# Reversed column order in the float32r products of a two-block decoder kernel, with the split weights at four relative places

## Chip, cores and metric

One core of a Trainium2 chip runs the whole program in one launch. The metric is the device time of that core in microseconds (us), from the first to the last instruction with what lies around them. Lower is better.

## What is computed

The reference is one layer of a hybrid decoder (a gated delta rule and a Mamba-2 mixer side by side, then a gated feed-forward with a short convolution), followed by a second block of two mixers (stick-breaking attention with multi-scale pooling; gated linear attention), each with its own feed-forward. There are 512 positions of 1,024 channels, in float32. Cut to what matters here:

```python
def hybrid_layer(x, ...):
    h = rms_norm(x, pre_mix_norm)
    proj = h @ w_in                                   # 1024 -> 6688
    ...                                               # delta rule and SSD, chunks of 64
    x = x + rms_norm(concatenate([o_a, o_s]) @ w_out, post_mix_norm)      # 2048 -> 1024
    h = rms_norm(x, pre_ffn_norm)
    u = causal_dwconv(h @ w_up, ffn_conv_w, ffn_conv_b)                   # 1024 -> 2 * 2816
    gate, up = split(u, 2)
    return x + rms_norm((silu(gate) * up) @ w_down, post_ffn_norm)        # 2816 -> 1024
# second block: an even mixer, a feed-forward, an odd mixer, a feed-forward,
# with the same kinds of products
```

Nearly all of the arithmetic is in these products of a weight matrix with an activation matrix of 512 columns.

## The kernel before

**Layout.** Activations lie channels by positions: a tile is 128 channels (partitions) by 512 positions, and a tensor of 1,024 channels is `KD` = 8 such tiles side by side. A weight matrix is cut into units. A unit makes 128 output channels: it is the stack of the 128x128 blocks that meet the input's tiles, 8 of them for an input of 1,024 channels (`KD`) and 11 for half of the 2,816 channels of the feed-forward (`HALF`). There are 305 units in the program.

**Exactness by splitting.** Both factors are split into two float32r parts, high and low. ScalarE rounds a unit to `whi` (L187), VectorE takes the remainder to `wlo` (L193), and the activations have such pairs too: `HH` and `HL`, `FH` and `FL` in the feed-forward, `MH`/`ML`, `PH`/`PL` and `DH`/`DL` in the mixers. TensorE then does three matrix products a block: high by high, high by low, low by high (L255 to L257 in `multiply`), and adds them up in one PSUM bank. Each is a weight load of 128x128 and a matmul that reads 512 columns of the activation tile (the moving operand) and writes 512 float32 columns of the bank. So a unit of `KD` is 24 matmuls, one of `HALF` 33.

**Where else the same product stands.** `fan` (L231 to L233) does two or three units side by side as the tiles of a normalised activation arrive, `begin_pe` (L1466 to L1468) does the same for the very first two units, and `mix_pe` (L2634 to L2636) is the output product of the first mixer. `busy` (L220) issues matmuls on split weights whose result nobody reads.

**The queue of weights.** SyncE loads each unit from HBM into one of four buffers `raw` (`RAW` = 4) once the unit four before it has been split. `whi` and `wlo` are two buffers each (`SPLIT` = 2), used in turn, so unit u + 2 is split when unit u is done (semaphore `unit_done`). Some units are split into tiles of their own ahead of time (`first_weights`, `early`).

**Places in SBUF.** `fixed` hands out addresses one after the other: parameters, `X`, `HH`, `HL`, four `raw`, two `whi`, two `wlo`, the constants `cst` (15 blocks of 128x128), `small`; all later tiles lie at `FREE` and beyond. A row of `whi` is 11 x 128 x 4 = 5,632 bytes, 11 times 512, and the tiles at `FREE` start a multiple of 512 bytes from `HH`. So every weight block and every activation tile that meet in a product start at the same remainder modulo 512 bytes.

**Order.** Each engine's instructions are written out stage by stage by hand; waits are on semaphores that count upward. What the change touches on the queues is the load of the constants in `load_l1`, L2190, behind the fourth weight unit. The semaphore `params_in` has counted all such loads when it reaches `ALL_PARAMS` = 16 x 9; TensorE waits for that at L1456, ScalarE and VectorE at the start of the first mixer (L2653, L2660).

## Time and profile before

| | |
|---|---|
| time of two runs | 2145.89 and 2153.01 us, median 2149.45 us |
| the profiled execution's own time | 2152.09 us |
| its span, first to last instruction | 2150.3 us |
| mean granted TensorE clock | 0.993 of full speed |
| instructions in the span | 26,841 |
| TensorE matmul (PE) | 2102.0 us busy, 98%, 9,776 |
| weight load (PEld) | 1702.9 us, 79%, 9,776 |
| VectorE (DVE) | 1212.8 us, 56% |
| ScalarE (ACT) | 905.8 us, 42% |
| GpSimd (POOL) | 325.0 us, 15% |
| DMA, share of 16 engines | 0.28, 88 GB/s |

How to read it. All times are of one execution. A row of the timeline gives the start of an instruction in us from the span's start, its duration, the engine, the line of the kernel, the operation and the names of what it writes and reads. The matmul's duration there contains the latency of a pipeline (0.39 us), while the next one starts 0.23 us after it: what a stream of matmuls costs is read from start to start. "128*128 128x512" is the size of the weights, and then what moves through them. PE and PEld are the same engine; the load for the next matmul runs beside the present one.

### The profile page before, as it was taken

The numbers are of one execution on the slowest core, as the hardware profiler recorded it, in microseconds if no ns is written. First come the engines' busy times: TensorE is split into PE (matmuls) and PEld (weight loads), VectorE is DVE, ScalarE is ACT, GpSimd is POOL, SyncE is SP. The second block draws the span as 40 slices with busy tenths as digits, with TensorE's granted clock in tenths as the row PEclk, the third lists the DMA queues.
The fourth block names the chain that finished last, engine by engine and source line by source line (L and its number), as shares of the span: only waits on it lengthen the run. The fifth ranks groups of instructions, "written<-read, shape, count | busy, mean of one in ns | idle before, by whom it ended". The sixth has DMA issues, their size and how long they took to land.

```text
span 2150.3 us, 26841 instructions
## 1 busy us (share of the span) xinstructions
PE 2102.0 (98%) x9776; PEld 1702.9 (79%) x9776; DVE 1212.8 (56%) x1663; ACT 905.8 (42%) x1282; POOL 325.0 (15%) x266
## 2 busy tenths in 40 slices
PE   6999999999999999999999999999999999999999
PEld 5778888878868888887766888888878878888887
DVE  5898755755366666225544566653354465666522
ACT  6883444434254444224555444442242254444421
POOL 0001121210112222001302122220000012222200
PEclk9999999999999999999999999999999999999999
DMA  7323222122223333222211333232222122333321
GB/s 235 93 77 93 75 75 79 49 69 69 91 66 98 98 98 115 99 80 69 66 43 40 98 98 96 93 119 95 86 69 89 60 70 97 98 97 96 116 95 66
DMA packets 81481, 188.96 MB, mean 88 GB/s; under 512 B 19824, under 2 KB 40432, under 8 KB 81392
## 3 DMA queue, kind: packets, MB, share of 16 engines
q1 hardware_dynamic: 81392, 187.75, 27.7%
q8 instruction: 59, 0.97, 0.2%
q14 instruction: 30, 0.25, 0.0%
HBM read 178.28 MB, written 9.44 MB: 87 GB/s over the span
## 4 chain that ended last, share of the span: by engine, by line
PE 91%; DVE 5%; ACT 2%; issue 1%; DMA 0%; POOL 0%; SPq 0%; DVEq 0%; ACTq 0%
PE acc L255 23%; PE acc L257 23%; PE acc L256 23%; PE bank L1247 1%; PE bank L231 1%; PE bank L233 1%; PE bank L232 1%; PE acc L2636 1%; PE acc L2634 1%; PE acc L2635 1%; PE bank L2019 1%; PE bank L1728 1%; DVE wlo L193 1%; PE bank L255 1%; PE bank L256 1%
## 5 line engine op out<-in xcount | busy, mean ns | idle before, releaser
L255 PE MATMUL acc<-HH,whi 128*128 128x512 f32 x1600 | 643.6, 402 | 6.9 <-DVE wlo L193 4.3
L257 PE MATMUL acc<-HH,wlo 128*128 128x512 f32 x1600 | 625.7, 391 | 0.0
L256 PE MATMUL acc<-HL,whi 128*128 128x512 f32 x1600 | 624.7, 390 | 0.0
L187 ACT ACTIVATE whi<-raw 128x1024 fp32r<-128x1024 f32 (+1 forms) x293 | 324.0, 1107 | 566.1 <-PE acc L257 536.8
L193 DVE TENSOR_TENSOR wlo<-raw,whi 128x1024 fp32r<-128x1024 f32 (+1 forms) x293 | 400.8, 1369 | 283.0 <-ACT whi L187 283.0
L255 PEld LDWEIGHTS acc<-HH,whi 128*128 128x128 f32 x1600 | 301.9, 189 | 73.8 <-DVE wlo L193 10.3
L257 PEld LDWEIGHTS acc<-HH,wlo 128*128 128x128 f32 x1600 | 301.2, 188 | 64.2
L256 PEld LDWEIGHTS acc<-HL,whi 128*128 128x128 f32 x1600 | 302.0, 189 | 62.6 <-issue 4.1
L255 PE MATMUL acc<-FH,whi 128*128 128x512 f32 x528 | 205.8, 390 | 0.0
L256 PE MATMUL acc<-FL,whi 128*128 128x512 f32 x528 | 205.4, 389 | 0.0
L257 PE MATMUL acc<-FH,wlo 128*128 128x512 f32 x528 | 205.4, 389 | 0.0
L390 DVE TENSOR_TENSOR acc<-acc,rs 128x512 f32<-128x512 f32 x150 | 104.8, 698 | 175.7 <-PE acc L257 175.7
L482 POOL TENSOR_TENSOR taps<-taps,taps 128x512 f32<-128x512 f32 x66 | 85.3, 1292 | 507.5 <-DVE taps L468 452.5
L447 ACT ACTIVATE FH<-taps 128x512 f32 (+1 forms) x66 | 41.8, 633 | 199.3 <-POOL taps L482 199.3
L255 PEld LDWEIGHTS acc<-FH,whi 128*128 128x128 f32 x528 | 99.1, 188 | 20.9 <-issue 0.2
L256 PEld LDWEIGHTS acc<-FL,whi 128*128 128x128 f32 x528 | 99.1, 188 | 20.8 <-issue 0.2
L257 PEld LDWEIGHTS acc<-FH,wlo 128*128 128x128 f32 x528 | 99.1, 188 | 20.5
L345 POOL TENSOR_TENSOR hn<-hn,sq 128x512 f32<-128x512 f32 x24 | 36.7, 1528 | 410.9 <-ACT sq L338 410.9
L468 DVE SCALAR_TENSOR_TENSOR taps<-acc,par,taps 128x510 f32<-128x510 f32 x117 | 87.6, 749 | 14.7 <-DVE taps L464 0.5
L487 POOL TENSOR_TENSOR FL<-taps,FH 128x512 f32 (+1 forms) x66 | 85.5, 1295 | 59.9 <-ACT FH L447 59.9
L438 ACT ACTIVATE taps<-acc,par 128x512 f32<-128x512 f32 x117 | 89.0, 761 | 0.6 <-DVE acc L390 0.6
L464 DVE SCALAR_TENSOR_TENSOR taps<-acc,par,taps 128x511 f32<-128x511 f32 x117 | 86.6, 740 | 0.0
(394 smaller groups left out, 2674.4 us busy)
## 6 DMA issues: line engine op xcount, KB each, us to landing
raw<-w SPq DMA_DIRECT2D x257, 512.0 KB, 3.5
raw<-w SPq DMA_DIRECT2D x48, 704.0 KB, 4.0
X<-x SPq DMA_DIRECT2D x4, 512.0 KB, 5.2
x_dram<-small SPq DMA_DIRECT2D x8, 256.0 KB, 4.7
xt_dram<-small SPq DMA_DIRECT2D x8, 256.0 KB, 4.5
a_dram<-l_am SPq DMA_DIRECT2D x8, 256.0 KB, 3.6
l_xt<-xt_dram SPq DMA_DIRECT2D x8, 256.0 KB, 3.3
l_x<-x_dram SPq DMA_DIRECT2D x8, 256.0 KB, 3.1
```

Source lines behind the costliest of these rows:

```text
L187: nc.scalar.activation(hi[:, 0:kt * P], raw[u % RAW][:, 0:kt * P], ACT.Copy).then_inc(w_hi_ready, 1)
L193: nc.vector.tensor_tensor(lo[:, 0:kt * P], raw[u % RAW][:, 0:kt * P], hi[:, 0:kt * P].bitcast(F32), ALU.subtract).then_inc(w_lo_ready, 1)
L255: nc.tensor.matmul(a[:, :], wh, tile(hi, k), start=start and k == 0, stop=False)
L256: nc.tensor.matmul(a[:, :], wh, tile(lo, k), start=False, stop=False)
L257: last = nc.tensor.matmul(a[:, :], wl, tile(hi, k), start=False, stop=stop and k == kt - 1)
L390: nc.vector.tensor_tensor(a[:, :], a[:, :], rs[:, :], ALU.mult).then_inc(scaled, 1)
L438: nc.scalar.activation(taps[j][:, :], a[:, :], ACT.Identity, scale=w(2), bias=w(3)).then_inc(tap_ready, 1)
L447: nc.scalar.activation(o, taps[j - 1][:, :], ACT.Copy).then_inc(fh_ready, 1)
L464: nc.vector.scalar_tensor_tensor(out=taps[j][:, 1:S], in0=a[:, 0:S - 1], scalar=w(1), in1=taps[j][:, 1:S], op0=ALU.mult, op1=ALU.add).then ...
L468: nc.vector.scalar_tensor_tensor(out=taps[j][:, 2:S], in0=a[:, 0:S - 2], scalar=w(0), in1=taps[j][:, 2:S], op0=ALU.mult, op1=ALU.add).then ...
L482: nc.gpsimd.tensor_tensor(taps[2 * b][:, :], taps[2 * b][:, :], taps[2 * b + 1][:, :], ALU.mult).then_inc(prod_ready, 1)
L487: nc.gpsimd.tensor_tensor(o, taps[2 * b][:, :], h.bitcast(F32), ALU.subtract).then_inc(f_ready, 1)
```

## The change

In the products named above, both the activation tile that is read and the PSUM bank that is written are given as `t[:, ::-1]`: the same elements with a step of -1, starting at column 511. Column j of the input still makes column j of the output. `busy`, and all products in plain float32, keep their order. The weight blocks are read as before.

The split weights get a row that is one block longer (12 x 128), and a unit starts in it at a shift: 0 or 64 elements for the units of 8 blocks (0 or 256 bytes, by buffer), 32 or 96 elements for those of 11 (128 or 384 bytes). The units with tiles of their own (`first_weights`, `early`) stay at shift 0.

To make room, `cst` shrinks from 15 to 10 blocks. The five left out (part of `level`) aren't read in the kernel before either. `FREE` moves down by 512 bytes.

```diff
-        whi = [fixed(f"whi{j}", [P, HALF * P], F32R) for j in range(SPLIT)]
-        wlo = [fixed(f"wlo{j}", [P, HALF * P], F32R) for j in range(SPLIT)]
-        cst = fixed("cst", [P, 15 * P])
+        whi = [fixed(f"whi{j}", [P, HALF * P + P], F32R) for j in range(SPLIT)]
+        wlo = [fixed(f"wlo{j}", [P, HALF * P + P], F32R) for j in range(SPLIT)]
+        SHIFT = {KD: (0, 64), HALF: (32, 96)}
+
+        def weights(w, kt):
+
+            o = SHIFT[kt][w]
+            return whi[w][:, o:o + kt * P], wlo[w][:, o:o + kt * P]
+
+        def flipped(t):
+
+            return t[:, ::-1]
+
+        cst = fixed("cst", [P, 10 * P])
...
-        NORM_COLUMNS, ALL_PARAMS = 9, 16 * 9
+        NORM_COLUMNS, ALL_PARAMS = 9, 16 * 10
...
-                wh, wl = whi[w][:, k * P:(k + 1) * P], wlo[w][:, k * P:(k + 1) * P]
-                nc.tensor.matmul(a[:, :], wh, tile(hi, k), start=start and k == 0, stop=False)
-                nc.tensor.matmul(a[:, :], wh, tile(lo, k), start=False, stop=False)
-                last = nc.tensor.matmul(a[:, :], wl, tile(hi, k), start=False, stop=stop and k == kt - 1)
+                wh, wl = (x[:, k * P:(k + 1) * P] for x in weights(w, kt))
+                nc.tensor.matmul(flipped(a), wh, flipped(tile(hi, k)), start=start and k == 0, stop=False)
+                nc.tensor.matmul(flipped(a), wh, flipped(tile(lo, k)), start=False, stop=False)
+                last = nc.tensor.matmul(flipped(a), wl, flipped(tile(hi, k)), start=False, stop=stop and k == kt - 1)
...
-                    sp.dma_start(cst[:, 2 * P:], cst_in[:, 2 * P:]).then_inc(params_in, 16)
+                    sp.dma_start(cst[:, 2 * P:5 * P], cst_in[:, 2 * P:5 * P]).then_inc(params_in, 16)
+                    sp.dma_start(cst[:, 5 * P:], cst_in[:, 10 * P:]).then_inc(params_in, 16)
```

`fan`, `begin_pe` and `mix_pe` are changed in the same way as `multiply`, and `split_hi` and `split_lo` write where `weights` says.

The only queue on which an instruction is added is SyncE's, near the start of the program. `raw` are the weights' buffers, `w` the weights in HBM, `par` and `cst` parameters and constants. Before:

```order
6 L2185 DMA raw_56<-w 128x1024
7 L2185 DMA raw_57<-w 128x1024
8 L2189 DMA par<-par 128x905
9 L2190 DMA cst<-cst 128x1664
10 L2192 DMA fold<-cst 32x32 x4
11 L2193 DMA tab_w<-w 128x8x32
12 L2185 DMA raw_54<-w 128x1024
```

The same place in the changed kernel, with its own line numbers:

```order
6 L2196 DMA raw_56<-w 128x1024
7 L2196 DMA raw_57<-w 128x1024
8 L2200 DMA par<-par 128x905
9 L2201 DMA cst<-cst 128x384
10 L2202 DMA cst<-cst 128x640
11 L2204 DMA fold<-cst 32x32 x4
12 L2205 DMA tab_w<-w 128x8x32
13 L2196 DMA raw_54<-w 128x1024
```

One load of 1,664 columns became two, of 384 and 640, and everything behind it stands one issue later. On TensorE, VectorE, ScalarE and GpSimd the same instructions stand in the same order in both kernels.

## Rows read from the trace of the kernel before

**Rows 1.** The page: busy time by engine, granted clock by slice, the last chain.

```profile
span 2150.3 us, 26841 instructions
PE 2102.0 (98%) x9776; PEld 1702.9 (79%) x9776; DVE 1212.8 (56%) x1663; ACT 905.8 (42%) x1282; POOL 325.0 (15%) x266
PEclk9999999999999999999999999999999999999999
PE 91%; DVE 5%; ACT 2%; issue 1%; DMA 0%; POOL 0%; SPq 0%; DVEq 0%; ACTq 0%
```

**Rows 2.** The page's DMA issues: weight units of 8 and of 11 blocks.

```profile
raw<-w SPq DMA_DIRECT2D x257, 512.0 KB, 3.5
raw<-w SPq DMA_DIRECT2D x48, 704.0 KB, 4.0
```

**Rows 3.** Timeline of PE and PEld, units of 8 blocks, full clock.

```profile
start us, us, engine line op out<-in xcount [idle before <-releaser]
699.85 0.39 PE L256 MATMUL acc<-HL,whi 128*128 128x512 f32 x1
...
702.57 0.39 PE L256 MATMUL acc<-HL,whi 128*128 128x512 f32 x1
...
699.86 0.19 PEld L257 LDWEIGHTS acc<-HH,wlo 128*128 128x128 f32 x1
```

**Rows 4.** Timeline of PE, units of 11 blocks, full clock.

```profile
900.00 0.39 PE L257 MATMUL acc<-FH,wlo 128*128 128x512 f32 x1
...
902.72 0.39 PE L257 MATMUL acc<-FH,wlo 128*128 128x512 f32 x1
```

**Rows 5.** Timeline of PE at 1.2 GHz, the first ten products.

```profile
17.93 0.63 PE L1467 MATMUL bank<-HL,early_hi 128*128 128x512 f32 x1
...
21.77 0.63 PE L1467 MATMUL bank<-HL,early_hi 128*128 128x512 f32 x1
```

**Rows 6.** Timeline of PE, plain float32 matmuls of 512 columns, full clock.

```profile
45.47 1.88 PE L1756 MATMUL bank<-l_sq,cst 128*128 128x512 f32 x4
47.18 0.94 PE L1766 MATMUL bank<-cst,t_ld 128*128 128x128 f32 x7
```

**Rows 7.** Timeline of PE, float32r products just after a gap, full clock.

```profile
59.64 0.40 PE L255 MATMUL acc<-HH,whi 128*128 128x512 f32 x1
59.88 0.39 PE L256 MATMUL acc<-HL,whi 128*128 128x512 f32 x1
60.10 0.39 PE L257 MATMUL acc<-HH,wlo 128*128 128x512 f32 x1
...
61.49 0.39 PE L257 MATMUL acc<-HH,wlo 128*128 128x512 f32 x1
```

**Rows 8.** Two stretches: us, then busy (count) by engine, clock, DMA share.

```profile
core 0: us, PE busy (x) PEld busy (x) DVE busy (x) ACT busy (x) POOL busy (x), PEclk, DMA share, GB/s
855.00:960.00 105.00, 105.00 (x465) 86.95 (x464) 28.71 (x23) 25.71 (x26) 9.45 (x8) 1.00 0.28 93
1750.00:1850.00 100.00, 100.00 (x439) 82.08 (x438) 55.65 (x63) 41.91 (x56) 22.29 (x16) 1.00 0.31 95
```

**Rows 9.** SyncE's queue near 10 us, the load's landing, and TensorE's first reader.

```profile
9.83 0.43 SPq L2190 DMA_DIRECT2D cst<-cst  x1
12.93 1.62 SPq L2185 DMA_DIRECT2D raw<-w  x1
...
cst<-cst SPq DMA_DIRECT2D x1, 832.0 KB, 7.1
...
29.57 1.92 PE L1459 MATMUL bank<-normed_x,tab_w 128*32 128x512 f32 x16
```

**Rows 10.** Groups by line: splitting on VectorE and ScalarE, with their idle time.

```profile
L193 DVE TENSOR_TENSOR wlo<-raw,whi 128x1024 fp32r<-128x1024 f32 (+1 forms) x293 | 400.8, 1369 | 283.0 <-ACT whi L187 283.0
L187 ACT ACTIVATE whi<-raw 128x1024 fp32r<-128x1024 f32 (+1 forms) x293 | 324.0, 1107 | 566.1 <-PE acc L257 536.8 <-PE acc L2636 11.9 <-PE bank L233 8.6
```

More of the change, by code:

```diff
@@ L97, in program @@
         ident, ones, upper, lower, halves = (cst[:, k * P:(k + 1) * P] for k in range(5))
-        neg_lower, neg_ones, hidden = (cst[:, k * P:(k + 1) * P] for k in range(12, 15))
-        level = [cst[:, (5 + k) * P:(6 + k) * P] for k in range(7)]
+        neg_lower, neg_ones, hidden = (cst[:, k * P:(k + 1) * P] for k in range(7, 10))
+        level = {5 + k: cst[:, (5 + k) * P:(6 + k) * P] for k in range(2)}
         def col(name, k=0, n=1):
@@ L181, in split_hi @@
         def split_hi(act, u, i, per, kt, first=None, behind=SPLIT):
-            hi = whi[u % SPLIT] if first is None else first[0]
+            hi = (weights(u % SPLIT, kt) if first is None else first)[0]
             act.wait_ge(raw_in[u % RAW], at(16 * (u // RAW + 1), i, 16 * per // RAW))
@@ L189, in split_lo @@
         def split_lo(dve, u, i, per, kt, first=None, behind=SPLIT):
-            hi, lo = (whi[u % SPLIT], wlo[u % SPLIT]) if first is None else first
+            hi, lo = weights(u % SPLIT, kt) if first is None else first
             dve.wait_ge(w_hi_ready, at(u + 1, i, per))
@@ L224, in fan @@
             u0, n = c["u"], c["fan"]
-            w = [c["first"][j] if j < 2 else (whi[(u0 + j) % SPLIT], wlo[(u0 + j) % SPLIT]) for j in range(n)]
+            w = [c["first"][j] if j < 2 else weights((u0 + j) % SPLIT, KD) for j in range(n)]
             pe.wait_ge(w_lo_ready, u0 + n)
@@ L1311, in sb_pe @@
             pe.wait_ge(w_lo_ready, u0 + 12)
-            busy(bank[0], whi[(u0 + 11) % SPLIT], 12)
+            busy(bank[0], weights((u0 + 11) % SPLIT, KD)[0], 12)
             for i in range(NP):
@@ L2632, in mix_pe @@
                         pe.wait_ge(h_ready, c["h"] - 2 * KD + h * KD + j + 1)
-                    wh, wl = whi[w][:, j * P:(j + 1) * P], wlo[w][:, j * P:(j + 1) * P]
-                    nc.tensor.matmul(a[:, :], wh, tile(hi, j), start=h == 0 and j == 0, stop=False)
-                    nc.tensor.matmul(a[:, :], wh, tile(lo, j), start=False, stop=False)
-                    last = nc.tensor.matmul(a[:, :], wl, tile(hi, j), start=False, stop=h == 1 and j == KD - 1)
+                    wh, wl = (x[:, j * P:(j + 1) * P] for x in weights(w, KD))
+                    nc.tensor.matmul(flipped(a), wh, flipped(tile(hi, j)), start=h == 0 and j == 0, stop=False)
+                    nc.tensor.matmul(flipped(a), wh, flipped(tile(lo, j)), start=False, stop=False)
+                    last = nc.tensor.matmul(flipped(a), wl, flipped(tile(hi, j)), start=False, stop=h == 1 and j == KD - 1)
                 last.then_inc(unit_done, 1)
```

18 lines of the change are left out of this document (9 added, 9 removed).

## Prediction

> **What bounds the kernel now.** I read the page first: TensorE's matmuls are busy 98% of the span, and the chain that ended last lies on PE for 91% of it [rows 1]. The granted clock is at its upper level in every slice [rows 1]. The other engines have room: in a stretch of the last feed-forward PE is busy 100 of 100 us, VectorE 56, ScalarE 42 [rows 8]. So the time is the number of matmuls by the time from one start to the next, and I looked next for both numbers.
>
> The number: 257 weight units of 8 blocks and 48 of 11 [rows 2] make 257 x 8 + 48 x 11 = 2,584 blocks, with three products each 7,752 matmuls, all of 512 columns. These are the ones that the change touches.
>
> The pace: in a steady stretch twelve of them take 702.57 - 699.85 = 2.72 us, 226.7 ns each [rows 3]. With 11-block units it is the same, 2.72 us for twelve [rows 4]. 7,752 x 226.7 ns = 1,757 us, 82% of the span of 2150.3 us. The rest (some 390 us: plain float32 products, waits, the start) isn't touched.
>
> At 2.4 GHz, 512 columns one a cycle are 213.3 ns. So each matmul pays 13.3 ns more than its columns, 7,752 x 13.3 = 103 us in all. That is the only amount that a mere change of order and place can win back, and what it consists of decides the case. Three views bear on it.
> - At 1.2 GHz nine steps take 21.77 - 17.93 = 3.84 us, 426.7 ns each, which is 512 / 1.2 GHz and nothing more [rows 5]. The surplus is there at full speed alone, so it isn't a fixed number of array cycles a matmul.
> - Plain float32 matmuls of 512 columns take (47.18 - 45.47) / 4 = 427.5 ns a pass at the full clock, 0.8 ns above two cycles a column [rows 6]. A stream that reads its columns at half the pace has no surplus either, although it loads weights as often.
> - After a gap the pace isn't 226.7 yet: eight steps take 61.49 - 59.64 = 1.85 us, 231 ns each, single ones about 240 and 220 [rows 7]. Same shape, same line, same places; the surplus depends on how the streams stand to each other.
>
> The weight load for the next matmul begins with the present matmul, 699.86 against 699.85 [rows 3]. My reading, argued and not shown: while 128 weight columns are fetched, the fetch of the moving columns at full pace is now and then held up. Then direction and relative place may matter, for better or worse. All weights and tiles of before stand at one relative place, so the trace has no row of another, and none with a step of -1.
>
> **The change, part by part.**
> 1. Reading the moving operand from column 511 down: 7,752 times, unknown price. From below: the surplus vanishes down to the 0.8 ns of [rows 6], so -12.5 ns each, -97 us. From above: one column in two cycles as at [rows 5], +200 ns each, +1,550 us. The step has the same size and the elements are neighbours as before, so the nearest row is the present one, [rows 3]. I take 0.
> 2. Writing PSUM from column 511 down: same count, same upper bound. A direction in itself has no reason to help the write. I take 0.
> 3. The four relative places: 0, 128, 256 and 384 bytes. Units of 8 blocks have 0 or 256 (2,056 blocks, 80%), those of 11 have 128 or 384 (20%). The nearest rows for another relation of the streams are [rows 7]: 231 ns, +4.6 each if all stayed there (+36 us), and about 240 ns for the single worst step. If half of the places gained 4 ns and half lost 4, the sum would be 0. I take 0, with the four as a spread that makes either extreme less likely.
> 4. The splits write to a shifted start. Sizes are unchanged; 1,369 ns on VectorE and 1,107 on ScalarE a unit, hidden below 24 x 226.7 = 5,440 ns of TensorE, with 283 and 566 us of idle time ahead of them [rows 10]. 0. If TensorE sped up to 214 ns a step, a unit would be 5,140 ns, still far above both.
> 5. One more load on SyncE's queue: 0.43 us [rows 9], and 832 KB become 512. The load before is issued at 9.83 us and lands 7.1 us later, at 17; TensorE's first wait for all parameters is ahead of the products at 29.57 [rows 9]. 12 us of cover. The next weight unit, issued at 12.93, comes 0.4 us later; it lies behind four that are loaded already. 0; without any cover it would be 0.5 us.
> 6. `FREE` moves by 512 bytes, the same remainder: 0.
>
> Sum: 0 on the profiled execution's own time of 2152.09 us (span 2150.3, 1.8 us around it). It lies 2.6 us above the median of the runs, so I give the median, 2149 us.
>
> A rule of the Trainium skill on PSUM (PSUM — Partial Sum Buffer, Specifications) speaks against the change: lines are 8 bytes, and any access that isn't contiguous slows matmuls significantly. No row here shows such an access. If a step of -1 counts as not contiguous the sum would go by the upper bound above. The page on SBUF (SBUF — State Buffer, Specifications) gives lines of 16 bytes and wants two hits in a line; read backward, float32 still has four. By that rule the read costs nothing, and the sum stays 0.
>
> **The rivals.**
> - *The streams get out of each other's way (faster).* Both fetches then meet less often, in one direction or at a shift. For it: [rows 5 to 7], which make the surplus a matter of how streams meet. Against it: 226.7 ns to the digit in two stages whose tiles lie far apart [rows 3, 4], which looks like a pattern that settles by itself whatever the place. All of the surplus gone gives 2149 - 97 = 2052 us, half of it 2149 - 48 = 2101. It passes over 2% when the mean step falls by 43 / 7.752 = 5.5 ns, to 221. Chance 0.33.
> - *They meet more often (slower).* The mechanism and place are the same, in the 7,752 steps. If every step were as the slow start [rows 7], +36 us, 2185, still within 2%. If the surplus doubled to 26.7 ns (240 ns a step, which single steps of [rows 7] reach), +103 us, 2252. It decides once the mean passes 226.7 + 5.5 = 232.2 ns. Chance 0.18 for over 2%.
> - *A step of -1 drops to one column in two cycles (much slower).* The price is that of [rows 5], whatever causes it, on the read or on the write: 426.7 ns a step, 2149 + 1,550 = 3,700 us. For it: rows of before never do this, and at 2.4 GHz a float32 stream needs neighbours fetched together. Against it: neighbours they still are. Chance 0.12. The rule of the PSUM page named above would make it this case.
> - *Nothing changes.* The two reads don't meet at all and the 13.3 ns belong to something in TensorE that neither direction nor place touches. 2149 us; with the mixtures in item 3 this is my forecast, 0.37. The Trainium skill (TensorE: Matmul & The Clock Gate, Step-by-step: what each phase is for) says that weight load and moving operand have independent read ports, by which the load takes nothing from the running matmul. By that rule the sum is 0; rows 5 to 7 don't bear it out fully, since the surplus varies with what runs beside.
>
> **How the numbers follow.** 2% is 43 us, about what a measurement of this kernel can tell from no change. Faster 0.33, within 2% 0.37, slower 0.18 + 0.12 = 0.30. The likeliest case has its own range, 2107 to 2192 us. The range for 8 in 10 takes in nearly all of the faster rival, down to 2055, and most of the milder slower one, up to 2235; it leaves out the 0.12 of the halved pace and some 0.05 at the ends.
>
> **What would show it.** The steps from start to start in the timeline: 226.7 ns in the steady stretches means nothing changed, below 221 the faster rival, above 232 the slower, near 427 the halved pace. The down stages (11 blocks) against all others tell places 128 and 384 from 0 and 256, and successive units tell the two buffers apart. If the first products of the span, at shift 0, move as much as the rest, it is the direction and not the place. Weight loads should stay at 0.19 us and the plain float32 products at 427.5 ns. TensorE's idle time should stay where it is; new idle time on it, for `wlo`, would say that something else than the pace moved. The prediction is wrong if the mean step leaves 221 to 232 ns.

## The result, and the profile after

| | before | after |
|---|---|---|
| median of two runs | 2149.45 us | 2193.4 us (2190.98 and 2195.82) |
| ratio, 95% interval | | 1.0204 [1.0117, 1.0292] |
| span of the profiled execution | 2150.3 us | 2189.2 us |
| mean granted TensorE clock | 0.993 | 0.996 |

The changed kernel is 2% slower: the loss is clear of the noise, and whether it is more or less than 2% the interval leaves open. The forecast was 2149 us with the likeliest case "nothing changes"; 2193 us lies inside the range of 2055 to 2235 us, but by the rival named "they meet more often", which had a chance of 0.18.

From the page of the kernel after: busy time by engine, the shares of the last chain, and the two groups that split weights (busy us, mean ns, then idle us and its releasers).

```profile
span 2189.2 us, 26842 instructions
PE 2143.5 (98%) x9776; PEld 1702.0 (78%) x9776; DVE 1215.1 (56%) x1663; ACT 905.1 (41%) x1282; POOL 319.6 (15%) x266
...
PE 91%; DVE 5%; ACT 2%; issue 1%; DMA 0%; POOL 0%; DVEq 0%; ACTq 0%
...
L198 ACT ACTIVATE whi<-raw 128x1024 fp32r<-128x1024 f32 (+1 forms) x293 | 323.6, 1105 | 599.2 <-PE acc L268 568.8
L204 DVE TENSOR_TENSOR wlo<-raw,whi 128x1024 fp32r<-128x1024 f32 (+1 forms) x293 | 402.3, 1374 | 279.0 <-ACT whi L198 279.0
```

Against [rows 1] PE has grown by 41.5 us with the same 9,776 matmuls. Weight loads, VectorE and ScalarE are within 2.5 us of before, GpSimd is 5 us lower, and the shape of the chain is the same. The splits take 1,105 and 1,374 ns against 1,107 and 1,369 [rows 10]; ScalarE waits 33 us longer for TensorE, which is the slower one.

Timeline of PE after: start, duration, line, what is written and read. First the same stages as in [rows 3] and [rows 4], then the first products of the span at full clock, then two at 1.2 GHz.

```profile
699.72 0.40 PE L266 MATMUL acc<-HH,whi 128*128 128x512 f32 x1
...
702.52 0.40 PE L266 MATMUL acc<-HH,whi 128*128 128x512 f32 x1
...
899.92 0.40 PE L266 MATMUL acc<-FH,whi 128*128 128x512 f32 x1
...
902.72 0.40 PE L266 MATMUL acc<-FH,whi 128*128 128x512 f32 x1
...
22.39 0.40 PE L1477 MATMUL bank<-HH,early_hi 128*128 128x512 f32 x1
...
27.99 0.40 PE L1477 MATMUL bank<-HH,early_hi 128*128 128x512 f32 x1
```

Twelve steps take 702.52 - 699.72 = 2.80 us in units of 8 blocks (places 0 and 256 bytes), 902.72 - 899.92 = 2.80 us in units of 11 (128 and 384 bytes), and 24 steps take 27.99 - 22.39 = 5.60 us in the first products, whose weights never left place 0. All three are 233.3 ns, against 226.7 before [rows 3, 4]. At 1.2 GHz three steps take 21.24 - 19.96 = 1.28 us, 426.7 ns, as in [rows 5]:

```profile
19.96 0.63 PE L1477 MATMUL bank<-HH,early_hi 128*128 128x512 f32 x1
...
21.24 0.63 PE L1477 MATMUL bank<-HH,early_hi 128*128 128x512 f32 x1
```

**The sum.** Over the whole trace, the mean of all steps below 270 ns between two such products is 227.27 ns before (the slower starts of [rows 7] included) and 233.40 ns after: 6.13 ns x 7,752 = 47.5 us. The mean clock gives some back: 0.996 x 2189 leaves 0.004 x 2189 x 2 = 17.5 us at 1.2 GHz (twice, since the lower level is half speed), before it was 0.007 x 2150 x 2 = 30.1 us, and half of the difference of 12.6 is 6 us. 47.5 - 6 gives some 41.5, which is what PE's busy time gained; the spans differ by 38.9 us and the medians by 44. So the place of the loss is one: every product's step.

SyncE's queue at the added load, and its landing (issue us, duration; then KB and us to landing):

```profile
10.16 0.44 SPq L2202 DMA_DIRECT2D cst<-cst  x1
...
cst<-cst SPq DMA_DIRECT2D x1, 320.0 KB, 6.0
```

The second load of the constants costs 0.44 us of the queue and lands 6.0 us after its issue, at 16.2 us; [rows 9] had one load landing at 17. Longest of TensorE's waits, after (engine line waited for: us in total, times, longest):

```profile
PE bank L283 <- DVE hn L312: 11.4, 1, 11.4
...
PE acc L266 <- DVE wlo L204: 4.9, 3, 2.9
```

The longest is a change of stage, and `wlo` counts for 4.9 us, against 5.4 before; no new wait stands here.

### The profile page after: what moved, and what is told of

Its sections match the earlier page's. It is cut to its first block, busy times and chain, and to the rows that moved or that the text cites. A ratio compares the mean times of both kernels' runs of the same rounds, so it can differ in the third digit from the quotient of the medians.

```text
span 2189.2 us, 26842 instructions
## 1 busy us (share of the span) xinstructions
PE 2143.5 (98%) x9776; PEld 1702.0 (78%) x9776; DVE 1215.1 (56%) x1663; ACT 905.1 (41%) x1282; POOL 319.6 (15%) x266
## 4 chain that ended last, share of the span: by engine, by line
PE 91%; DVE 5%; ACT 2%; issue 1%; DMA 0%; POOL 0%; DVEq 0%; ACTq 0%
PE acc L266 23%; PE acc L267 23%; PE acc L268 23%; PE bank L1258 1%; PE bank L242 1%; PE acc L2647 1%; PE bank L243 1%; PE bank L244 1%; PE acc L2648 1%; PE acc L2646 1%; PE bank L2030 1%; PE bank L1739 1%; PE bank L266 1%; DVE wlo L204 1%; PE bank L267 1%
## 5 line engine op out<-in xcount | busy, mean ns | idle before, releaser
L266 PE MATMUL acc<-HH,whi 128*128 128x512 f32 x1600 | 654.8, 409 | 6.1 <-DVE wlo L204 3.8
L267 PE MATMUL acc<-HL,whi 128*128 128x512 f32 x1600 | 637.6, 398 | 0.0
L268 PE MATMUL acc<-HH,wlo 128*128 128x512 f32 x1600 | 637.3, 398 | 0.0
L198 ACT ACTIVATE whi<-raw 128x1024 fp32r<-128x1024 f32 (+1 forms) x293 | 323.6, 1105 | 599.2 <-PE acc L268 568.8
L204 DVE TENSOR_TENSOR wlo<-raw,whi 128x1024 fp32r<-128x1024 f32 (+1 forms) x293 | 402.3, 1374 | 279.0 <-ACT whi L198 279.0
L266 PE MATMUL acc<-FH,whi 128*128 128x512 f32 x528 | 210.2, 398 | 0.0
L267 PE MATMUL acc<-FL,whi 128*128 128x512 f32 x528 | 209.8, 397 | 0.0
L268 PE MATMUL acc<-FH,wlo 128*128 128x512 f32 x528 | 209.8, 397 | 0.0
```

The lines of the kernel that those rows point to most:

```text
L198: nc.scalar.activation(hi[:, 0:kt * P], raw[u % RAW][:, 0:kt * P], ACT.Copy).then_inc(w_hi_ready, 1)
L204: nc.vector.tensor_tensor(lo[:, 0:kt * P], raw[u % RAW][:, 0:kt * P], hi[:, 0:kt * P].bitcast(F32), ALU.subtract).then_inc(w_lo_ready, 1)
L266: nc.tensor.matmul(flipped(a), wh, flipped(tile(hi, k)), start=start and k == 0, stop=False)
L267: nc.tensor.matmul(flipped(a), wh, flipped(tile(lo, k)), start=False, stop=False)
L268: last = nc.tensor.matmul(flipped(a), wl, flipped(tile(hi, k)), start=False, stop=stop and k == kt - 1)
```

## The experiments

The change has three parts that touch a product: the direction of the read, the direction of the write, and the weights' place. The explanations to tell apart were: the read stream meets the fetch of weights more often when it runs backward (the mechanism of the second rival); the write to PSUM pays; the places pay. Behind them stood the question of what the surplus over 213.3 ns consists of, since a kernel that avoids it would be faster than both.

Two kinds of kernels were run. The full kernel with one part of the change was timed against the kernel before, which was run again beside it each time; the ratios are to those runs. Kernels of single forms issue long streams of one form of product on fixed tiles and nothing else; they compute nothing of the reference. Of each form, 40 products settle, then 48 are recorded as one row, whose time is 47 steps and one matmul's own 0.38 to 0.40 us. So a row of 11.04 us is (11.04 - 0.39) / 47 = 226.6 ns a step, and one of 11.36 is (11.36 - 0.40) / 47 = 233.2; the steps below are worked out from unrounded rows.

### Order alone, places alone, and the whole change again

```diff
 # order_alone: the kernel after, with
-        SHIFT = {KD: (0, 64), HALF: (32, 96)}
+        SHIFT = {KD: (0, 0), HALF: (0, 0)}
 # place_alone: the kernel after, with
-            return t[:, ::-1]
+            return t[:, :]
```

> The changed kernel with all shifts at 0: the reversed order alone, weights at one relative place. Theory A (the order of the moving read meets the weight fetch more often, whatever the place): steps of 233.3 ns as in the changed kernel, time the same as it, about 2193 us, ratio to before 1.02. Theory B (the four places did it, the order is free): steps back to 226.7 ns, time about 2149 us. Theory C (the reversed write to PSUM did it): the same as A here, so this run doesn't tell A from C.

> The changed kernel with columns in ascending order on both sides: the four places alone, and the constants' load in two parts. Theory A (order): steps of 226.7 ns, time within 0.5% of before, 2149 us. Theory B (places): steps of 233.3 ns, about 2193 us; if only some places cost, the stages with 11-block units would differ from the others. Theory C (reversed write): 226.7 ns as A.

> The changed kernel as it is, for a narrower interval beside the two others on the same chip: ratio to before 1.02 (7,752 steps of 6.7 ns more are 52 us, less what TensorE's clock gives back).

| | us | ratio to before |
|---|---|---|
| order alone | 2193.67 | 1.0202 [1.0181, 1.0223] |
| places alone | 2161.52 | 1.0036 [1.0020, 1.0051] |
| whole change again | 2189.95 | 1.0189 [1.0167, 1.0211] |

Timeline of PE, order alone, units of 11 blocks:

```profile
899.73 0.40 PE L268 MATMUL acc<-FH,wlo 128*128 128x512 f32 x1
...
902.53 0.40 PE L268 MATMUL acc<-FH,wlo 128*128 128x512 f32 x1
```

Timeline of PE, places alone: units of 8 blocks, then of 11.

```profile
700.04 0.39 PE L267 MATMUL acc<-HL,whi 128*128 128x512 f32 x1
...
702.76 0.39 PE L267 MATMUL acc<-HL,whi 128*128 128x512 f32 x1
...
899.97 0.40 PE L268 MATMUL acc<-FH,wlo 128*128 128x512 f32 x1
...
902.75 0.40 PE L268 MATMUL acc<-FH,wlo 128*128 128x512 f32 x1
```

The order alone gives all of the loss: 12 steps in 2.80 us, 233.3 ns, with all places as before. The places alone leave the units of 8 blocks at 2.72 us (226.7 ns; places 0 and 256 bytes) and lift those of 11 to 2.78 us (231.7 ns here, 232.4 over the stage; places 128 and 384 bytes). 48 units x 33 products = 1,584 products x 5.7 ns = 9 us; the spans of the two traces differ by 10.9 us, and the ratio says 8 us, from 4 to 11. The two don't add up: with the read reversed, units of 11 blocks cost 233.3 ns at place 0 and at the shifted ones.

### Single forms: read or write, lines or elements

```diff
 # bench_a, some of its forms, each in a stream of its own (mv: moving, wt: weights, a: PSUM bank)
+  L73   mm(a, wt[:, 0:P], mv[:, 0:S])                       # as before
+  L80   mm(a, wt[:, 0:P], rev(mv[:, 0:S]))                  # read reversed
+  L87   mm(rev(acc[0]), wt[:, 0:P], mv[:, 0:S])             # written reversed
+  L94   mm(rev(acc[0]), wt[:, 0:P], rev(mv[:, 0:S]))        # both, as after
+  L248  mm(acc[0][:, 0:256], wt[:, 0:P], rev(mv[:, 0:256])) # 256 columns, read reversed
+  L276  mm(a, wt[:, 0:P], grouped(mv[:, 0:S], 4))           # groups of 4 backward, inside forward
+  L304  mm(a, wt[:, 0:P], grouped(mv[:, 0:S], 4, 1, -1))    # groups of 4 forward, inside backward
+  L318  mm(a, wt[:, 0:P], mv[:, 0:2 * S:2])                 # every second element
```

> A kernel of its own that leaves out the whole computation: runs of 88 equal matmuls each, 40 to settle and 48 to read the step from start to start, one form after the other, with four short float32 passes between forms. Theory A (weight fetch against moving read): base 226.7 ns; moving read reversed alone 233.3; PSUM write reversed alone 226.7; both 233.3; weights of 64 and 32 columns cost a half and a quarter of the surplus of 13.3 ns; 256 and 384 columns of moving operand the same surplus of 13.3 (120 and 173 ns); bfloat16 about 216 in both directions; moving operand shifted, or weights shifted, by less than a block: either no difference or one that repeats with 4 or 8 elements. Other orders of the moving columns (pairs, fours, blocks of 8 or 32 in descending order) lie between 226.7 and 233.3. Theory C (write): write reversed alone 233.3, read reversed alone 226.7. Theory D (a fixed cost in the array that a reversed pattern makes larger by setup): surplus independent of weight columns, and a swap of halves costs as much as a full reversal.

Timeline of PE, one row for 48 products of each form:

```profile
38.95 11.04 PE L73 MATMUL acc<-mv,wt 128*128 128x512 f32 x48
59.61 11.36 PE L80 MATMUL acc<-mv,wt 128*128 128x512 f32 x48
80.35 11.04 PE L87 MATMUL acc<-mv,wt 128*128 128x512 f32 x48
101.02 11.36 PE L94 MATMUL acc<-mv,wt 128*128 128x512 f32 x48
547.06 5.84 PE L248 MATMUL acc<-mv,wt 128*128 128x256 f32 x48
614.72 11.36 PE L276 MATMUL acc<-mv,wt 128*128 128x512 f32 x48
698.40 11.04 PE L304 MATMUL acc<-mv,wt 128*128 128x512 f32 x48
748.53 21.83 PE L318 MATMUL acc<-mv,wt 128*128 128x512 f32 x48
```

Read row by row: the reversed read costs 6.7 ns (L80), the reversed write nothing (L87), both together as much as the read alone (L94). Reversing four elements within a group of 16 bytes is free (L304), while taking the groups backward, forward inside, costs the full 6.7 ns (L276). So it is the order of 16-byte groups that counts. Every second element takes 451 ns a step, half the pace (L318).

The price of going backward holds for 512 columns and isn't the same at other lengths. With 256 columns the reversed read took 118.4 ns (L248) against 120.0 forward, which is faster; with 384 it took 177.7 against 173.3. Forward, the surplus over the columns was 13.3 ns at 256, 384 and 512 columns alike and 16.0 at 448, so it isn't in proportion to the columns either.

The Trainium skill (SBUF — State Buffer, Specifications) gives SBUF lines of 16 bytes and wants neighbours to be read together; L304 and L276 agree with lines of that size. It asks for two hits in a line for the full rate; L318 has two in each and runs at half the pace, so for float32r the runs differ from the page. What it implied for this change, that a backward read with four hits in each line is free, holds for the elements in a line and fails for the lines' order. The Trainium skill (PSUM — Partial Sum Buffer, Specifications) has any access that isn't contiguous slow a matmul significantly; with a step of -1 on the write the runs show no cost at all (11.04 us at L87 as at L73).

In the same kernel bfloat16 products took 215.8 ns in either direction, and plain float32 ones 429.2 ns a pass in either. Shortening the weights to 64 or 32 columns, with loads of 134 and 108 ns instead of 188, gave 230.1 and 231.7 ns. A half and a quarter of the surplus had been expected; it grew, so it isn't in proportion to the weight columns fetched.

### Single forms: which places and which orders

```diff
 # bench_b: weights at 22 places forward and 32 backward, moving tiles at 4, both shifted together, and the blocks' order
+  L129  mm(a, wt[:, 32:32+P], mv[:, 0:S])
+  L136  mm(a, wt[:, 36:36+P], mv[:, 0:S])
+  L185  mm(a, wt[:, 64:64+P], mv[:, 0:S])
+  L465  mm(a, wt[:, 4:4+P], mv[:, 4:4+S])
+  L486  mm(a, wt[:, 32:32+P], mv[:, 32:32+S])
```

> A kernel of its own that leaves out the whole computation: 82 forms of the float32r matmul, 88 each, as in the first such kernel. Theory A1 (the relation of the two start addresses decides, with a period of 256 bytes): in ascending order a shift of the weights by 64, 128, 192 or 256 elements gives 226.7 ns, all others 230 to 234; shifting weights and moving operand by the same amount gives 226.7 again; moving alone by 64 or more 226.7. Reversed: 233.3 at multiples of 64, up to 236.7 between, and no place back at 226.7. Theory A2 (each operand's own alignment decides): shifting both by the same amount stays at 231 to 234. Theory A3 (some place of the reversed order is better than the ascending one): at least one of the 32 reversed shifts is below 226.7. Order of moving columns: blocks of 64 elements in descending order 226.7 by A1 (their period), blocks of 16 about 233.

Timeline of PE, the five forms above:

```profile
205.51 11.32 PE L129 MATMUL acc<-mv,wt 128*128 128x512 f32 x48
226.19 11.04 PE L136 MATMUL acc<-mv,wt 128*128 128x512 f32 x48
371.29 11.04 PE L185 MATMUL acc<-mv,wt 128*128 128x512 f32 x48
1210.02 11.36 PE L465 MATMUL acc<-mv,wt 128*128 128x512 f32 x48
1271.64 11.05 PE L486 MATMUL acc<-mv,wt 128*128 128x512 f32 x48
```

Weights 128 bytes on cost 5.8 ns (L129), weights 256 bytes on nothing (L185), and both streams 128 bytes on nothing either (L486; so with 8, 16 and 64 elements). Both streams 16 bytes on did cost, 233.3 ns (L465), and both 8 bytes on 231.1. Of the 22 places of the weights, read forward, the multiples of 256 bytes and one other (36 elements, L136) were at 226.7 ns, all others from 228.3 to 234.4; places that differ by 256 bytes gave the same step. So what counts is mostly the place of one read stream against the other, modulo 256 bytes, as theory A1 has it. L465 is what theory A2 expected, so each stream's own place has a part too. Reversed, none of 32 places was below 233.3, and some were at 236.7. At 32 elements it was 236.7 in bench_a and 233.3 here, so one form can keep two paces. Going backward over blocks of 32 columns or fewer cost 233.3; over blocks of 64 columns (256 bytes) or more, forward inside, nothing: 226.7.

```diff
 # bench_c: a moving stream that reads few lines again and again; spread weights
+  L87   mm(a, wt[:, 0:P], mv[:, 0:4].unsqueeze(1).to_broadcast([P, 128, 4]))
+  L122  mm(a, wt[:, 0:P], mv[:, 0:64].unsqueeze(1).to_broadcast([P, 8, 64]))
+  L178  mm(a, wt[:, 0:8 * P:8], mv[:, 0:S])
```

> A kernel of its own that leaves out the whole computation: 45 forms, 88 matmuls each. Theory A (the surplus comes from the fetch of weights and the fetch of moving columns meeting in SBUF): a moving operand that repeats one column or one line of 16 bytes has a smaller surplus than 13.3 ns, or a much larger one where it stays on the line of the weights; weights 8 elements apart (128 lines in place of 32) raise it above 30 ns (244 ns a step was seen) in either direction; bfloat16 stays at 216 at all shifts of the weights, and rises only when its weights or its moving columns are spread over as many lines as float32 has; plain float32 stays at 429. Theory E (the surplus is a fixed 13.3 ns of TensorE at full clock, and addresses only add to it): one-column and one-line moving operands stay at 226.7, never below, at every shift; float32r never falls below 226.7 in any form of 512 columns.

Timeline of PE, the three forms above:

```profile
78.78 10.66 PE L87 MATMUL acc<-mv,wt 128*128 128x512 f32 x48
181.13 11.04 PE L122 MATMUL acc<-mv,wt 128*128 128x512 f32 x48
346.69 11.87 PE L178 MATMUL acc<-mv,wt 128*128 128x512 f32 x48
```

A moving stream that reads one 16-byte line 128 times has a step of 218.7 ns (L87). One that walks through the same 16 lines (256 bytes) eight times is at 226.7, exactly as the full tile (L122), and at 233.3 when reversed. Two lines gave 217.8, four 242.1, eight 236.7. Weights 8 elements apart, so that each column comes from a line of its own, take 244.0 ns (L178); 4 elements apart, also a line each, they took 234.9 in bench_b. So the surplus depends on where both streams read, as meetings of the two fetches would make it, and a walk that repeats after 256 bytes costs what the full tile costs.

A bfloat16 stream of every second element, which passes through as many lines as a float32r tile, took 225.9 ns forward and 231.1 backward, where neighbouring elements took 215.8 in either direction. So the order of lines isn't a matter of float32r alone.

```diff
 # bench_d: the moving columns in several passes; the best:
+  L227  mm(a, wt[:, 0:0+P], mv[:, 0:S].rearrange("p (a t f) -> p t a f", t=4, f=8))
```

> A kernel of its own that leaves out the whole computation: 43 single forms in other orders of the moving lines, and nine streams with the kernel's own triple of products (two tiles, two weight blocks) at shifts 0, 32, 36 of the weights, ascending and reversed, entered after a gap or behind another stream. Theory A1: what counts is the sequence of line numbers modulo 16, so whole turns of 16 lines in ascending order give 226.7 ns and descending lines inside blocks of 64 give 233.3 with blocks in any order; strides of 16 lines and more, which stay on one number, are slow or fast, unlike either. If any order is below 226.7 ns, a kernel faster than both exists. Triples: 226.7 at shift 0 and 233.3 reversed, as in the kernels; shift 36 gives 226.7 in the stream of one form and 233.0 in the full kernel, so if the triple alone gives 233 it is the three products that differ, and if it gives 226.7 after a gap and 233 behind another stream it is how the stream is entered.

Timeline of PE, that form:

```profile
540.20 10.72 PE L227 MATMUL acc<-mv,wt 128*128 128x512 f32 x48
```

Here the first pass takes columns 0 to 7, 32 to 39, 64 to 71 and so on, the second 8 to 15, 40 to 47, ..., in four passes. It has a step of (10.72 - 0.38) / 47 = 220.0 ns. Others went either way: groups of 4 columns in four passes 226.9, lines 8 apart 247, 16 apart 278, 32 apart 268. With the read plain and the write in one of two other orders (lines 16 apart, lines backward) it was 226.7.

### Two candidates in the full kernel

```diff
 # blocks64: the kernel after at shift 0, blocks of 64 columns backward, forward inside
-            return t[:, ::-1]
+            return t[:, :].rearrange("p (a b) -> p a b", b=64)[:, ::-1, :]
 # shift36: the kernel after with plain order, and every shared unit 36 elements on
-        SHIFT = {KD: (0, 64), HALF: (32, 96)}
+        SHIFT = {KD: (36, 36), HALF: (36, 36)}
-            return t[:, ::-1]
+            return t[:, :]
```

> The changed kernel with all shifts at 0, and in place of the full reversal the eight blocks of 64 columns in descending order, ascending inside, on the read and on the write. Theory A1 (the relation of the two read streams modulo 256 bytes decides, which blocks of 64 elements keep): steps of 226.7 ns and the time of before, 2150 us, within 0.4%. If any departure from one ascending run of 512 columns costs (a setup per pattern or per direction): steps of 233 ns and some 2190 us.

> Ascending order, all split weights in the two shared buffers at a shift of 36 elements: the only other shift below 64 that gave 226.7 ns in the kernel of single forms. If that carries over, the steady step is 226.7 ns and the time that of before within 0.4%; if entries into a stream settle sooner there than at shift 0, where they take 229.4 ns in the first mixer, up to 0.2% less than before, 2147 us. If it doesn't carry over, 230 to 234 ns a step and 2180 to 2200 us.

Blocks of 64: 2151.80 us, 1.0001 [0.9986, 1.0017]. Shift 36: 2188.43 us, 1.0186 [1.0162, 1.0210].

Timeline of PE, blocks of 64:

```profile
699.96 0.39 PE L266 MATMUL acc<-HH,whi 128*128 128x512 f32 x1
...
702.68 0.39 PE L266 MATMUL acc<-HH,whi 128*128 128x512 f32 x1
```

Timeline of PE, shift 36:

```profile
699.89 0.39 PE L266 MATMUL acc<-HH,whi 128*128 128x512 f32 x1
...
702.69 0.39 PE L266 MATMUL acc<-HH,whi 128*128 128x512 f32 x1
```

The first carries over: the read begins with the last 64 columns and ends with the first, and 12 steps still take 2.72 us. This is the sharpest statement on the change: running from the end to the start isn't what costs, running backward inside 256 bytes is. The second doesn't carry over. A form with 226.7 ns as a long stream has 233.3 in the kernel (2.80 us), so the form alone doesn't fix the step.

### The kernel's own three products, and four passes in the full kernel

```diff
 # bench_e: 54 streams of the kernel's triple (high by high, low by high, high by low), each behind a gap, in other orders and places
 # turns: the kernel after at shift 0, with
-            return t[:, ::-1]
+            return t[:, :].rearrange("p (a t f) -> p t a f", t=4, f=8)
```

> A kernel of its own that leaves out the whole computation: 54 streams of the kernel's triple of products, 66 matmuls each after a gap, in orders that take groups of 4, 8, 16 or 32 columns in 2, 4 or 8 passes, at shifts of the weights from 0 to 60 elements. Expected by theory A: groups of 8 in four passes 220 ns at shift 0 and 64-periodic, 229 to 230 at 16 and 32; groups of 4 in four passes 226 to 227; groups of 8 in eight passes 233 to 250; plain ascending 226.7. A step below 220 at some shift would be a still better version.

> The changed kernel with all shifts at 0 and another column order, on the read and the write: groups of 8 columns (two lines) taken 32 columns apart, four passes over the 512. As a single form it took 220.0 ns a step, 6.7 less than ascending. Theory A (the sequence of lines against the weight fetch decides): if the kernel's triples hold that phase, 7,752 x 6.7 = 52 us less than before, about 2100 us, ratio 0.976. If the triples settle in another phase, as at shift 36, steps between 220 and 234 and a time between 2100 and 2200 us. A fixed price of any order but ascending would give 2190 us or more.

Of the triples the four passes of 8 columns at place 0 were again the lowest, 219.98 ns; all others, the same passes at other places among them, lay from 226.3 to 258.8. In the full kernel they gave 2161.64 us, 1.0063 [1.0042, 1.0084], slower than before although faster than after.

Timeline of PE, four passes, in the mixer's output stage, in the first feed-forward, and later:

```profile
560.17 0.38 PE L2646 MATMUL acc<-DH,whi 128*128 128x512 f32 x1
...
562.81 0.38 PE L2646 MATMUL acc<-HH,whi 128*128 128x512 f32 x1
...
699.47 0.39 PE L266 MATMUL acc<-HH,whi 128*128 128x512 f32 x1
...
702.24 0.39 PE L266 MATMUL acc<-HH,whi 128*128 128x512 f32 x1
...
1021.77 0.38 PE L266 MATMUL acc<-HH,whi 128*128 128x512 f32 x1
...
1023.53 0.38 PE L268 MATMUL acc<-HH,wlo 128*128 128x512 f32 x1
```

Twelve steps take 2.64 us (220.0 ns) at 560 us and 2.77 us (230.8 ns) at 699 us, with the same instruction on the same tiles. Between them TensorE waited 3.5 us once, at 629 us, and ran 3 us at 1.2 GHz; from there to 980 us the step stayed at 230 to 231. It isn't a change for good: the eight steps from 1021.77 take 1.76 us, 220.0 ns each again, behind a few short float32 passes. The trace changes between the two several times in the mixers, while the three feed-forwards stay at 230.7. The same form has two steady paces.

### What chooses the pace

Two answers were possible: the stream before decides it, and it then holds (P), or it drifts with what else runs in the kernel (Q).

```diff
 # bench_f: 120 products of a form, each time behind another entry (a gap, plain, reversed, a shifted stream, float32, bfloat16)
 # turns_mixed: as turns, but the first block of every unit in plain order
+            return t[:, :] if k == 0 else t[:, :].rearrange("p (a t f) -> p t a f", t=4, f=8)
```

> A kernel of its own that leaves out the whole computation: 39 streams of 120 products in the kernel's triple, each entered in one of eight ways (after a gap, behind a plain, reversed or shifted stream, behind two streams in passes at shifts 36 and 44, behind long float32 passes, behind bfloat16). Theory P (a stream keeps one of several steady phases, and the entry picks it): the order in four passes shows 220.0 behind some entries and about 230.7 behind others, shift 36 shows 226.7 behind some and 233.3 behind others, and plain ascending at shift 0 shows 226.7 behind all. Streams whose units begin with one or two plain blocks (mixed) take the same phase whatever the entry, at 220 to 223 ns if the plain block leads into the fast phase, at 229 to 231 if not. Theory Q (the kernel's later stages are slow for another reason, their places or their DMAs): each stream has one step, independent of the entry.

> As the run in four passes of groups of 8 columns, but the first block of every unit in plain ascending order. Theory P with a plain block leading into the fast phase: 7/8 of the steps at 220.0 and 1/8 at 226.7 in all stages, 7,752 x 5.8 = 45 us less than before, about 2105 us. If the plain block leads into the slow phase, or the mixture has a phase of its own: 227 to 231 ns a step, 2150 to 2185 us.

Timeline of PE in the streams' kernel: four passes behind a gap, then the same behind 24 plain products, both after over 100 products of their own.

```profile
54.32 0.38 PE L73 MATMUL acc<-mv,wt 128*128 128x512 f32 x1
...
55.64 0.38 PE L73 MATMUL acc<-mv,wt 128*128 128x512 f32 x1
...
87.82 0.39 PE L85 MATMUL acc<-mv,wt 128*128 128x512 f32 x1
...
89.20 0.39 PE L85 MATMUL acc<-mv,wt 128*128 128x512 f32 x1
```

Six steps take 1.32 us (220.0 ns) in the one and 1.38 us (230.0; 230.6 over the last 48) in the other. Four passes keep 220.0 behind a gap or a stream with weights 32 elements on, and 230.6 to 230.8 behind plain, reversed, float32 or bfloat16 products and behind two streams of four passes at other places. Weights 36 elements on keep 226.7 behind plain or reversed products and 233.3 behind all else. Plain order at place 0 comes to 226.7 behind anything. With nothing else running, the pace is set by the entry: P. It bears on shift 36 as well, with one thing left open. The stream of one form that gave 226.7 ns (L136) stood behind two short float32 products, and the kernel's triple behind such products kept 233.4 in bench_d and here; it kept 226.7 only directly behind a plain or reversed stream. So the two steady paces of shift 36 are shown, and the kernel runs in the slower one; whether the one form differed by its single tile and block or by what ran ahead of the float32 products, no run separates.

Plain order in the first block as a way to lead each unit into the good pace failed: 2167.47 us, 1.0084 [1.0061, 1.0106], mean step 229.9 ns. In the streams the same mixture kept 230.7 to 230.9 behind six of the eight entries.

### A block that leads into the good pace

```diff
 # bench_g: units of one leading block and seven in four passes, behind five entries; L74 is the best lead
 # turns_led: the kernel after at shift 0, with
-        def flipped(t):
-            return t[:, ::-1]
+        def flipped(t, k=1):
+            if k == 0:
+                return t[:, :].rearrange("p (a t f) -> p a t f", t=2, f=32)[:, :, ::-1, :]
+            return t[:, :].rearrange("p (a t f) -> p t a f", t=4, f=8)
```

> A kernel of its own that leaves out the whole computation: 50 streams of five units of 24 products in the order of four passes, where the first block of each unit (the first two in one form) is in another order: neighbours of 32, 16, 8 or 4 columns swapped, or two, four or eight passes of other group sizes; each entered in five ways. By theory P a first block that disturbs the slow phase but not the fast one brings every entry to (3 x 233 + 21 x 220) / 24 = 221.6 ns a step; the swap of neighbours of 32, which stands to the weights as a shift of 32 does and led into 220.0 before, is the likeliest. If all forms stay at 229 to 231 behind some entry, no such first block is found here, and the slow phase is the stabler one.

> The full kernel in the order of four passes, all shifts at 0, with the first block of each unit (one block in eight in the fans, in four in units that are done by parts) read with neighbouring groups of 32 columns swapped. Theory P: 221.7 ns a step in all stages, as in the streams of single forms from every entry; 7,752 x 5.0 = 39 us less than before, about 2110 us, ratio 0.982; a little more in units of 11 blocks (221.2 ns). If waits and short float32 passes inside the stages bring the slow phase back in part: 222 to 228 ns, 2115 to 2160 us. If DMAs or places of the kernel matter beside the entry: 230 ns as without the first block, some 2165 us.

Of the leading blocks tried, one gave the good pace from every one of the five entries: the columns in groups of 32, each two neighbouring groups swapped. Timeline of PE, that stream, its leading block in two successive units:

```profile
46.51 0.40 PE L74 MATMUL acc<-mv,wt 128*128 128x512 f32 x1
...
51.83 0.40 PE L74 MATMUL acc<-mv,wt 128*128 128x512 f32 x1
```

24 steps take 5.32 us, 221.7 ns each. Other leads gave 223.6 to 235 by entry. In the full kernel, with that lead in each unit of 8 or 11 blocks (one block in four where a unit is done by parts, one in eight where units run side by side):

Timeline of PE, four passes with a lead, units of 8 blocks; then the leading block.

```profile
699.08 0.38 PE L270 MATMUL acc<-HH,whi 128*128 128x512 f32 x1
...
701.72 0.38 PE L270 MATMUL acc<-HH,whi 128*128 128x512 f32 x1
...
702.38 0.40 PE L270 MATMUL acc<-HH,whi 128*128 128x512 f32 x1
...
703.08 0.38 PE L270 MATMUL acc<-HH,whi 128*128 128x512 f32 x1
```

2128.91 us, ratio 0.9907 [0.9881, 0.9933]: 0.9% faster than before, clear of the noise, and about 3% faster than the kernel after. That is half of what 221.7 ns in all stages would have given; it lies in the range expected if waits and short float32 passes bring the slow pace back in part. Twelve steps take 2.64 us (220.0 ns), and the lead's three take 703.08 - 702.38 = 0.70 us (233 ns). Over 640 to 850 us the mean step is 222.5 ns. It isn't as low everywhere: 226.0 in the units of 11 blocks, some of which run in the slow pace and come back, and 225.8 in the first mixer with its gaps. The mean of the trace is 223.9, against 227.27 before: 3.4 x 7,752 = 26 us, of which 21.8 arrived in the span. The steps of 270 ns and more, left out of these means, take 102.0 us against 95.5 before and account for the difference; why they are longer wasn't looked into.

## Why the prediction went as it did

The forecast was "nothing changes", and its own sign of being wrong, a mean step outside 221 to 232 ns, came: 233.4.

1. **What bounds the kernel.** This held. The number of products by their step explains the result to some 3 us, and TensorE's idle time stayed where it was (48 us of the span before, 46 after).
2. **Item 1, the reversed read, priced at 0.** This step failed. It costs 6.67 ns a product (233.33 against 226.66 alone, 233.3 against 226.7 in the kernel), and 7,752 x 6.67 = 51.7 us is the loss before the clock and the slow starts give some back. The bounds of -97 and +1,550 us held it, but the argument for the value did not. (The lower bound was itself a little too far: plain float32 passes in a long stream took 429.2 ns, so their surplus is 2.5 ns and not the 0.8 of [rows 6].) It said that the step has the same size and the elements are neighbours as before, so the nearest row is the present one. But the elements within a line aren't what the order touches; the lines are, and they stand in another relation to the weights' lines. I had written ahead of it that direction and place may matter in just this way, and had rows 7 as the nearest for another relation of the streams: 231 to 240 ns. The nearest row for a reversed read was there and not in the steady stretch. The reason against that rival, 226.7 ns to the digit in two stages "whatever the place", was weak: in both stages everything lay at one relative place, so the digit said nothing on another.
3. **Item 2, the reversed write, at 0.** Shown: 226.66 ns alone.
4. **Item 3, the places, at 0.** Right for 80% of the blocks (226.7 at 0 and 256 bytes) and wrong for 20% (232.4 at 128 and 384), 9 us if the order is plain: the spread of four places contained no gain. In the changed kernel it adds nothing: 2189.95 us for the whole change, 2193.67 for the order alone, with intervals that overlap. Half gaining and half losing was not what happened.
5. **Items 4 to 6.** Splits at the same times, one load more at 0.44 us and hidden, `FREE` without effect: as said.
6. **The rivals.** "They meet more often" had the place right, a longer step in all 7,752 products, and its cause as far as the runs go: the order of the read does it, while the meeting itself isn't shown. Its deciding point of 232.2 ns lies just below the 233.3 found; I gave it 0.18 and the outcome fell at its edge. So the measured time is inside the range by the width left for this rival, not by the forecast's working. "Nothing changes" is refuted. For it stood the Trainium skill (TensorE: Matmul & The Clock Gate, Step-by-step: what each phase is for), by which weight load and moving operand have ports of their own. For float32r the runs speak against the load taking nothing: moving only the weights, by 128 bytes, costs 5.8 ns a product. They don't show by what way. Halved pace did not come with a step of -1; it came with a step of 2 (451 ns). "Faster" didn't come in this change, but its half did: the surplus can be lowered, from 13.3 to 6.7 ns, by an order of lines that suits.
7. **What would show it.** All the marks named did their work: the step above 232, the same in both stages (so not the place), the same in the first products at shift 0 (so the direction), loads at 0.19 us, no new idle time for `wlo`.

**What stays open.** That the two fetches meet is supported and not shown: the surplus follows the relation of the two streams modulo 256 bytes, is lowest where the moving stream reads one or two lines, is highest where lines are far apart, and is absent at 1.2 GHz. bfloat16 (215.8 ns) and plain float32 (429.2) stay 2.5 ns above 213.3 and 426.7 in both directions and at all places of the weights tried. But the surplus isn't in proportion to the number of weight columns, both streams moved 16 bytes together cost 6.7 ns, and why four lines in turn are worse than one or eight, or why 256 columns are read faster backward, I can't say. That the pace has more than one steady value, chosen in the streams by the entry, is shown; what state of the chip holds it is not.

## To carry to other kernels

Where TensorE is the bound, read the step from start to start to a tenth of a nanosecond over a dozen products, and treat whatever it has above its columns as something that addresses and order can move either way; 6.7 ns on 7,752 products was 2% of this kernel. Start float32r weights and moving tiles at multiples of 256 bytes, and with 512 columns don't read the moving tile backward within 256 bytes; the write to PSUM cost nothing in any order tried. And measure a form in the kernel's own sequence of products and as the kernel will enter it: a long stream of one form told 226.7 ns for a shift of 36 elements where the kernel had 233.3.

## What the runs showed of the hardware

- The commonest steady steps of 512 float32r columns at 2.4 GHz were 220.0, 226.7 and 233.3 ns, that is 528, 544 and 560 cycles: 512 and one, two or three times 16. Other forms lie between, below (217.8 for two lines again and again) or above (up to 281 ns for lines 16 apart).
- Groups of 16 bytes are the unit of the moving read: order within one is free (226.7 ns), order between them counts (233.3 backward), and not across blocks of 256 bytes (226.7). With 256 columns backward is the faster one, 118.4 against 120.0.
- bfloat16 products of 512 columns took 215.8 ns whatever the order's direction and the weights' place, float32 ones 429.2 ns a pass. With every second element they took 225.9 forward and 231.1 backward.
- One form on the same tiles can run at two steady paces (220.0 and 230.7, or 226.7 and 233.3), by what ran before it. In the full kernel in four passes the pace went from the first to the second at a wait of 3.5 us, and came back some 390 us later behind short float32 passes.
